# Opening of a transformer block: three products of the first scale half on VectorE, and two weight tiles loaded ahead of the second scale half

## The chip, the cores and the metric

The kernel runs on one core of one Trainium2 chip. The metric is device time in microseconds (us), the median of several executions. TensorE is PE in all rows, VectorE is DVE, ScalarE is ACT, GpSimd is POOL, and SyncE is SP.

## The reference, cut to what matters

The block takes x (512 tokens by 1024 channels) and one conditioning vector c, all float32. It is a feed-forward layer, a mixer of attention heads, and a second feed-forward layer. Each of the three normalizes its input and modulates it. The opening concerns the first one only:

```python
cond  = silu(c)                                   # 1024 values
ada   = cond @ w_ada + b_ada                      # 9 blocks of 1024: shift, scale, gate of three layers
h     = rmsnorm(x, g) * (1.0 + scale) + shift     # g: g_ffn1
gate, up = split(h @ w_up, 2)                     # 1024 -> 2 * 2816
x     = x + 0.5 * gate_0 * ((silu(gate) * up) @ w_down)
```

So nothing of the first weight product can be made before shift and scale of its channels are there, and these need 1024 by 2048 values of w_ada, 8 MB.

## The kernel before, in words

**Precision.** A float32 weight tile of 128 columns is split into a high part (`w_hi`, rounded by ACT) and a low part (`w_lo`, the rest, by DVE), and so is h (`h_hi`, `h_lo`). Each product is then three matmuls of 512 columns (`three`, lines 885 to 889). A tile is `[128, 8, 128]`: all eight groups of 128 channels for 128 output columns.

**Shift and scale in four pieces.** The 1024 channels are worked in two halves of 512. `load_piece(p)` (line 781) loads one quarter of the first two blocks of `w_ada` with four DMAs of 512 KB, each holding two of the eight groups of input channels. The pieces are called `SCALE_A`, `SCALE_B`, `SHIFT_A` and `SHIFT_B`; A is the half of channels 0 to 511. There are two ways in which the sum over the 1024 input channels is made:

- Shift, on DVE: `piece_product` (line 1944) multiplies 128 by 512 values by one column of `cond` and adds to `ada_acc`, eight times. Then `shift_columns` on PE (line 911) sums over the partitions, by four float32 matmuls of the accumulator with a column of ones. One float32 matmul stands in the trace as two records.
- Scale, on PE: `scale_row` (line 894) is a float32 matmul of 128 by 512 for each of the eight groups, with `cond` as the stationary operand. ACT copies the row that comes out (`keep_line`, line 1544). `scale_columns` (line 903) turns it into a column with four small matmuls.

DVE adds the bias (`piece_sum`, line 1957), makes the amplitude (`first_amp`, line 1962), and then `h_full` and `h_low_first` on DVE and `h_first` on ACT make `h_hi` and `h_lo` of one group of 128 channels after the other.

**The order of the opening** is written out by hand on each queue, and each engine does its list strictly in order:

- SP issues the DMAs: x in four, SHIFT_A, SCALE_A, SCALE_B (four each), the weight tiles 0, 1 and 2 (`load_up_first`, line 771), SHIFT_B, tile 3 (lines 788 to 796).
- PE transposes x, and x scaled by its norm (`turn_xr`), with the eight products of SCALE_A among them. Then come `shift_columns(SHIFT_A)`, the first product of SCALE_B, `scale_columns(SCALE_A)`, the last two `turn_xr`, and products 1 to 5 of SCALE_B (lines 968 to 983). A product of even number waits for its DMA (line 897). Then the weight tiles 0 and 1 with groups 0 to 3 (lines 993 to 998), products 6 and 7 of SCALE_B, tiles 2 and 3, and after them groups 4 to 7.
- ACT copies the transposes out, keeps the line, and makes `h_hi` of groups 0 to 3 with the high parts of tiles 0 and 1 in between (lines 1562 to 1575).
- DVE makes the eight products of SHIFT_A, the sums, then `h` of groups 0 to 3 with the low parts of tiles 0 and 1 in between (lines 2114 to 2131), then the products of SHIFT_B.

PE starts a weight tile only when `w_lo` of it is there (`split_ready`, line 891). After the opening, PE works through the rest of the block nearly without pause.

Of the kernel before, what the change touches and what calls it, by code (L numbers as in the profile page):

```python
# [5 lines left out]
ALU = mybir.AluOpType  # L6
# [7 lines left out]
P = 128  # L14
SEQ = 512
TB = SEQ // P
D = 1024
KC = D // P
# [13 lines left out]
B_LOOP = 2  # L32
XR_BANK = (5, 6, 7, 0, 1, 2, 3, 0)
SCALE_A, SCALE_B, SHIFT_A, SHIFT_B = range(4)
UP_BLOCKS = (FC - 2) // 4
DOWN_CHUNKS = (3, 3, 2, 0)

# [263 lines left out]
def hybrid_block_kernel(  # L301
# [4 lines left out]
    with ctx:  # L306
        def sem(name):
            return ctx.enter_context(nc.semaphore(name))
# [14 lines left out]
        def keep(name, shape, dt=F32):  # L323
# [17 lines left out]
        ones = keep("ones", [P, 1])  # L341
# [6 lines left out]
        cond = keep("cond", [P, KC])  # L348
# [19 lines left out]
        ada_acc = at("ada_acc", [P, D], F32, region + 2 * FC * SEQ * 4 + 2 * D * 4)  # L368
# [6 lines left out]
        ada_first = at("ada_first", [P, 4, KC, SEQ], F32, region + 2 * TB * D * 4)  # L375
# [79 lines left out]
        bank = [ctx.enter_context(nc.psum_tensor(f"bank{i}", [P, SEQ], F32)) for i in range(8)]  # L455
# [4 lines left out]
        piece_in, up_in = block_in, block_in[0:3]  # L460
# [20 lines left out]
        silu_done, hid_f32, hid_hi_done, hid_done = (  # L481
            sem("silu_done"), sem("hid_f32"), sem("hid_hi_done"), sem("hid_done"))
        mix_zero, k_zero = sem("mix_zero"), sem("k_zero")
        k_twice = [sem("k_twice0"), sem("k_twice1")]
        wf_split, wf_split_hi, f_logit, f_sum, f_act, f_dve = (
            sem("wf_split"), sem("wf_split_hi"), sem("f_logit"), sem("f_sum"), sem("f_act"), sem("f_dve"))
# [272 lines left out]
        def _(sp):  # L759
# [11 lines left out]
            def load_up_first(n):  # L771

                c0 = n // 2 * P + n % 2 * FFN
                sp.dma_start(tile8(w_raw, n), up_v[0][:, :, c0:c0 + P]).then_inc(w_in_sem[n], 16)
# [6 lines left out]
            def load_piece(p):  # L781

                c0 = (p < 2) * D + p % 2 * SEQ
                for n in range(KC // 2):
                    sp.dma_start(ada_first[:, p, 2 * n:2 * n + 2, :], ada_v[:, 2 * n:2 * n + 2, c0:c0 + SEQ])\
                      .then_inc(piece_in[p][n], 16)
# [2 lines left out]
                sp.dma_start(x_nat[:, tb, :], x[0, tb * P:(tb + 1) * P, :]).then_inc(x_in[tb], 16)  # L789
            load_piece(SHIFT_A)  # L790
            load_piece(SCALE_A)
            load_piece(SCALE_B)
            for n in range(3):
                load_up_first(n)
            load_piece(SHIFT_B)
            load_up_first(3)
            sp.dma_start(b_f[:], b_forget.rearrange("o h -> h o")).then_inc(fbias_in, 16)
# [84 lines left out]
        def _(pe):  # L882
            mm = nc.tensor.matmul
# [10 lines left out]
            def scale_row(p, k):  # L894

                if k % 2 == 0:
                    pe.wait_ge(piece_in[p][k // 2], 16)
                last = mm(bank[4 + p][:], cond[:, k:k + 1].broadcast_to([P, P]), ada_first[:, p, k, :],  # L898
                          start=k == 0, stop=k == KC - 1)
                if k == KC - 1:  # L900
                    last.then_inc(row_up, 1)

            def scale_columns(p):

                pe.wait_ge(row_kept, p + 1)
                for j in range(4):
                    last = mm(bank[7 - 3 * p][:, j:j + 1], scale_line[0:1, p, j * P:(j + 1) * P], ones[0:1, :],
                              start=True, stop=True)
                last.then_inc(ada_col, 1)

            def shift_columns(p):
# [56 lines left out]
            for k in range(3):  # L968
                turn_xr(k)
            pe.wait_ge(cond_ready, 1)  # L970
            for k in range(KC):
                scale_row(SCALE_A, k)
                if k < 3:
                    turn_xr(k + 3)
# [33 lines left out]
            for k in range(4, KC):  # L1008
                pe.wait_ge(h_done, k + 1)
                for n in range(2):  # L1010
                    last = tile_chunk(T_UP1, n, k, w2_hi, w2_lo)
                    if k == KC - 1:
                        last.then_inc(w_used, 1)
            for n in range(2, 4):
                for k in range(4, KC):
                    last = tile_chunk(T_UP1, n, k, w2_hi, w2_lo)
# [44 lines left out]
            n = KC - 1  # L1061
# [4 lines left out]
            for k in range(DOWN_PARTS[0][1]):  # L1066
                for h in range(2):
                    last = three(side_bank[h], tile8(w_hi, t % 2)[:, k, :], tile8(w_lo, t % 2)[:, k, :],
                                 hid_hi[:, k, side(h)], hid_lo[:, k, side(h)], k == 0, False)
# [44 lines left out]
            for k in range(KC):  # L1114
                pe.wait_ge(h_done, KC + k + 1)
                for i in range(2):
                    last = first_tiles(i, k, 1)
# [280 lines left out]
        def _(act):  # L1398
# [131 lines left out]
            def keep_xr(k):  # L1530

                act.wait_ge(xr_turned, k + 1)
                if k == 0:
                    act.wait_ge(x_turned, KC)
                a(xr[:, k, :], bank[XR_BANK[k]][:], ACT.Copy).then_inc(xr_ready, 1)

            def split_up(n):

                act.wait_ge(w_in_sem[n], 16)
                if n == 2:  # L1540
                    act.wait_ge(xr_turned, KC)
                a((w_hi if n < 2 else w2_hi)[:, n % SPLIT, :], w_raw[:, n, :], ACT.Copy).then_inc(w_hi_done, 1)

            def keep_line(p):

                act.wait_ge(row_up, p + 1)
                a(scale_line[0:1, p, :], bank[4 + p][0:1, :], ACT.Copy).then_inc(row_kept, 1)

            def h_first(k):

                act.wait_ge(ada_out, 2 if k < 4 else 4)
                act.wait_ge(amp_done, 1 if k < 4 else 2)
                a(h_hi[:, k, :], xr[:, k, :], ACT.Identity, bias=ada[:, k:k + 1], scale=amp[:, k:k + 1])\
                    .then_inc(h_hi_done, 1)
# [6 lines left out]

            for k in range(6):
                keep_xr(k)
            keep_line(SCALE_A)
            h_first(0)
            keep_xr(6)
            h_first(1)
            keep_xr(7)
            split_up(0)
            h_first(2)  # L1570
            split_up(1)
            h_first(3)
            split_up(2)
            split_up(3)
# [329 lines left out]
        def _(dve):  # L1904
# [39 lines left out]
            def piece_product(p, k):  # L1944

                c0 = p % 2 * SEQ
                if k % 2 == 0:
                    dve.wait_ge(piece_in[p][k // 2], 16)
                if k == 0:
                    ins = v.tensor_scalar(ada_acc[:, c0:c0 + SEQ], ada_first[:, p, 0, :], cond[:, 0:1], None, ALU.mult)  # L1950
                else:
                    dve.wait_ge(ada_mul, KC * (p - 2) + k)
                    ins = v.scalar_tensor_tensor(ada_acc[:, c0:c0 + SEQ], ada_first[:, p, k, :], cond[:, k:k + 1],
                                                 ada_acc[:, c0:c0 + SEQ], ALU.mult, ALU.add)
                ins.then_inc(ada_mul, 1)

            def piece_sum(order, c0, b):

                dve.wait_ge(ada_col, order)
                v.tensor_tensor(ada[:, c0:c0 + 4], bank[b][:, 0:4], vcol[:, c0:c0 + 4], ALU.add).then_inc(ada_out, 1)  # L1960
# [107 lines left out]
            def split_up(n):  # L2068

                dve.wait_ge(w_hi_done, n + 1)  # L2070
                hi, lo = (w_hi, w_lo) if n < 2 else (w2_hi, w2_lo)
                v.tensor_tensor(lo[:, n % SPLIT, :], w_raw[:, n, :], hi[:, n % SPLIT, :].bitcast(F32), ALU.subtract)\
                    .then_inc(w_lo_done, 1)
# [40 lines left out]
            dve.wait_ge(cond_ready, 1)  # L2114
            for k in range(KC):
                piece_product(SHIFT_A, k)
            piece_sum(1, 0, 6)
            piece_sum(2, KC, 7)
            first_amp(0)
            dve.wait_ge(amp_done, 1)  # L2120
# [3 lines left out]
            h_low_first(0)  # L2124
            h_low_first(1)
            h_full(2)
            split_up(0)
            h_low_first(2)
            split_up(1)
            h_full(3)  # L2130
            h_low_first(3)
            for k in range(4):
# [478 lines left out]
```

## Time and profile before

| what | value |
|---|---|
| median of 3 executions | 1090.0 us (1089.26 to 1090.44) |
| the profiled execution's own time | 1089.68 us |
| its span, first to last instruction | 1087.9 us |
| around the span | 1.78 us |
| PE busy | 1070.9 us, 98% |
| DVE busy | 691.8 us, 64% |
| ACT busy | 500.9 us, 46% |
| mean granted TensorE clock | 0.999 |

The profiled execution lies 0.3 us below the median. Durations in the rows further down are from this one execution. A busy share is an average over the whole span; the opening, which the change touches, is the first 50 us of it.

### The profile page before, as it was taken

The numbers are of one execution on the slowest core, as the hardware profiler recorded it, in microseconds if no ns is written. First come the engines' busy times: TensorE is split into PE (matmuls) and PEld (weight loads), VectorE is DVE, ScalarE is ACT, GpSimd is POOL, SyncE is SP. The second block draws the span as 40 slices with busy tenths as digits, with TensorE's granted clock in tenths as the row PEclk, the third lists the DMA queues.
The fourth block names the chain that finished last, engine by engine and source line by source line (L and its number), as shares of the span: only waits on it lengthen the run. The fifth ranks groups of instructions, "written<-read, shape, count | busy, mean of one in ns | idle before, by whom it ended". The sixth has DMA issues, their size and how long they took to land.

```text
span 1087.9 us, 16282 instructions
## 1 busy us (share of the span) xinstructions
PE 1070.9 (98%) x6072; PEld 911.4 (84%) x6072; DVE 691.8 (64%) x1054; ACT 500.9 (46%) x833; POOL 42.3 (4%) x76
## 2 busy tenths in 40 slices
PE   8999999999999999999999999999999999999997
PEld 5788888888878889888778777789999999978886
DVE  3755555555653557886786676678766667684343
ACT  5523222223222235776796776358544454541222
POOL 1000000000000001110111011000000000000000
PEclk9999999999999999999999999999999999999999
DMA  9868888885474552398699567246777667132221
GB/s 344 239 211 292 264 276 283 275 306 156 140 228 130 176 157 79 90 221 203 142 187 197 124 145 165 77 125 156 190 200 193 171 181 203 60 106 98 87 97 78
DMA packets 209053, 191.84 MB, mean 176 GB/s; under 512 B 7660, under 2 KB 183900, under 8 KB 206940
## 3 DMA queue, kind: packets, MB, share of 16 engines
q1 hardware_dynamic: 201392, 146.86, 45.8%
q0 software_dynamic: 7424, 44.04, 16.1%
q8 instruction: 42, 0.69, 0.3%
q14 instruction: 23, 0.19, 0.1%
q10 hardware_dynamic: 172, 0.06, 0.0%
HBM read 186.74 MB, written 44.04 MB: 212 GB/s over the span
## 4 chain that ended last, share of the span: by engine, by line
PE 89%; DVE 4%; DMA 2%; ACT 2%; issue 1%; SPq 0%; DVEq 0%; POOL 0%; ACTq 0%
PE bank L887 27%; PE bank L889 27%; PE bank L888 27%; PE bank L1246 1%; PE bank L898 1%; PE bank L1218 1%; DVE hid_lo L2066 1%; PE bank L1194 1%; PE bank L1195 1%; DMA x_nat<-in_x_dram 1%; DMA k_hh_b<-k_hh_b 0%; PE bank L924 0%; ACT w_hi L1411 0%; DMA k_hh_a<-k_hh_a 0%; DVE y L2584 0%
## 5 line engine op out<-in xcount | busy, mean ns | idle before, releaser
L887 PE MATMUL bank<-h_hi,w_hi 128*128 128x512 f32 (+1 forms) x592 | 230.3, 389 | 0.1
L889 PE MATMUL bank<-h_hi,w_lo 128*128 128x512 f32 (+1 forms) x592 | 223.5, 378 | 0.0
L888 PE MATMUL bank<-h_lo,w_hi 128*128 128x512 f32 (+1 forms) x592 | 223.5, 378 | 0.0
L1912 DVE TENSOR_TENSOR w_lo<-w_raw,w_hi 128x1024 fp32r<-128x1024 f32 x97 | 118.7, 1225 | 156.1 <-ACT w_hi L1411 155.5
L1411 ACT ACTIVATE w_hi<-w_raw 128x1024 fp32r<-128x1024 f32 x97 | 102.5, 1058 | 204.0 <-PE bank L889 179.2
L887 PEld LDWEIGHTS bank<-h_hi,w_hi 128*128 128x128 f32 x592 | 111.8, 189 | 25.5 <-issue 4.2
L888 PEld LDWEIGHTS bank<-h_lo,w_hi 128*128 128x128 f32 x592 | 111.7, 189 | 24.0 <-issue 2.9
L889 PEld LDWEIGHTS bank<-h_hi,w_lo 128*128 128x128 f32 x592 | 111.6, 189 | 22.6
L2018 DVE TENSOR_TENSOR up_lo<-up_raw,up_hi 128x1024 fp32r<-128x1024 f32 x80 | 86.6, 1085 | 21.1 <-ACT up_hi L1480 21.1
L889 PE MATMUL bank<-combo,up_lo 128*128 128x256 f32 x320 | 90.6, 283 | 0.0
L887 PE MATMUL bank<-combo,up_hi 128*128 128x256 f32 x320 | 90.6, 283 | 0.0
L888 PE MATMUL bank<-combo,up_hi 128*128 128x256 f32 x320 | 90.2, 282 | 0.0
L1480 ACT ACTIVATE up_hi<-up_raw 128x1024 fp32r<-128x1024 f32 x80 | 75.2, 943 | 0.0
L887 PE MATMUL bank<-hid_hi,w_hi 128*128 128x512 f32 (+1 forms) x198 | 74.0, 374 | 1.0 <-DVE w_lo L1912 1.0
L889 PE MATMUL bank<-hid_hi,w_lo 128*128 128x512 f32 (+1 forms) x198 | 73.5, 371 | 0.0
L888 PE MATMUL bank<-hid_lo,w_hi 128*128 128x512 f32 (+1 forms) x198 | 73.4, 371 | 0.0
L889 PE MATMUL bank<-w_hi,hid_lo 128*128 128x512 f32 x176 | 69.8, 396 | 0.0
L887 PE MATMUL bank<-h_hi,up_hi 128*128 128x256 f32 x240 | 68.0, 283 | 0.0
L888 PE MATMUL bank<-h_lo,up_hi 128*128 128x256 f32 x240 | 67.7, 282 | 0.0
L889 PE MATMUL bank<-h_hi,up_lo 128*128 128x256 f32 x240 | 67.6, 282 | 0.0
L1421 ACT ACTIVATE w_hi<-down_raw 128x1024 fp32r<-128x1024 f32 (+1 forms) x24 | 23.7, 987 | 86.6 <-PE bank L889 82.0
L1941 DVE SCALAR_TENSOR_TENSOR ada_acc<-ada_w,cond,ada_acc 128x1024 f32<-128x1024 f32 x49 | 62.6, 1278 | 0.0
(274 smaller groups left out, 2173.5 us busy)
## 6 DMA issues: line engine op xcount, KB each, us to landing
w_sums<-in_w_ffn_up_dram POOLq DMA_DIRECT2D x24, 1280.0 KB, 8.9
ada_w<-in_w_ada_dram SPq DMA_DIRECT2D x56, 512.0 KB, 3.8
w_raw<-in_w_ffn_up_dram SPq DMA_DIRECT2D x48, 512.0 KB, 7.2
up_raw<-w_sums SPq DMA_DIRECT2D x40, 512.0 KB, 5.5
w_raw<-in_w_in_dram SPq DMA_DIRECT2D x28, 512.0 KB, 3.8
w_sums<-w_sums POOLq DMA_DIRECT2D x8, 1280.0 KB, 10.3
up_raw<-in_w_ffn_up_dram SPq DMA_DIRECT2D x20, 512.0 KB, 4.1
down_raw<-in_w_ffn_down_dram SPq DMA_DIRECT2D x20, 512.0 KB, 3.7
```

The lines of the kernel that those rows point to most:

```text
L887: mm(dst, wh, xh, start=start, stop=False, skip_group_check=skip)
L888: mm(dst, wh, xl, start=False, stop=False, skip_group_check=skip)
L889: return mm(dst, wl, xh, start=False, stop=stop, skip_group_check=skip)
L898: last = mm(bank[4 + p][:], cond[:, k:k + 1].broadcast_to([P, P]), ada_first[:, p, k, :], start=k == 0, stop=k == KC - 1)
L1194: mm(zb[:, c0:c0 + n], qs, k_hh[j % 2][:, h, 0:n], start=True, stop=False)
L1195: mm(zb[:, c0:c0 + n], qs, k_l[j % 2][:, h, 0:n], start=False, stop=False)
L1411: a(w_hi[:, s, :], w_raw[:, r, :], ACT.Copy).then_inc(w_hi_done, 1)
L1421: a(w_hi[:, t % SPLIT, 0:n], down_raw[:, t % RAW, 0:n], ACT.Copy).then_inc(w_hi_done, 1)
L1480: a(up_hi[f % 2][q][:], up_raw[n % 3][q][:], ACT.Copy).then_inc(w_hi_done, 1)
L1912: v.tensor_tensor(w_lo[:, s, :], w_raw[:, r, :], w_hi[:, s, :].bitcast(F32), ALU.subtract)\
L1941: ins = v.scalar_tensor_tensor(ada_acc[:], source, cond[:, k:k + 1], ada_acc[:], ALU.mult, ALU.add)
L2018: v.tensor_tensor(up_lo[s][q][:], up_raw[s][q][:], up_hi[f % 2][q][:].bitcast(F32), ALU.subtract)\
```

## The change

It has three parts. PE makes the first five of the eight products of SCALE_A; DVE makes the other three after those of SHIFT_A, in the second half of `ada_acc`. `scale_columns(SCALE_A)` waits for them on a new semaphore and sums them over the partitions with four more float32 matmuls, into the same bank columns. SP issues the weight tiles 0 and 1 between SCALE_A and SCALE_B. ACT and DVE split tiles 0 and 1 before they make h, not between the groups of h.

```diff
+ON_PE = (5, 8)
@@ semaphores
+        scale_rest = sem("scale_rest")
@@ SP
             load_piece(SHIFT_A)
             load_piece(SCALE_A)
+            load_up_first(0)
+            load_up_first(1)
             load_piece(SCALE_B)
-            for n in range(3):
-                load_up_first(n)
+            load_up_first(2)
             load_piece(SHIFT_B)
             load_up_first(3)
@@ PE, scale_row
                 last = mm(bank[4 + p][:], cond[:, k:k + 1].broadcast_to([P, P]), ada_first[:, p, k, :],
-                          start=k == 0, stop=k == KC - 1)
-                if k == KC - 1:
+                          start=k == 0, stop=k == ON_PE[p] - 1)
+                if k == ON_PE[p] - 1:
                     last.then_inc(row_up, 1)
@@ PE, scale_columns
                 pe.wait_ge(row_kept, p + 1)
+                if p == SCALE_A:
+                    pe.wait_ge(scale_rest, KC - ON_PE[p])
                 for j in range(4):
                     last = mm(bank[7 - 3 * p][:, j:j + 1], scale_line[0:1, p, j * P:(j + 1) * P], ones[0:1, :],
-                              start=True, stop=True)
+                              start=True, stop=p == SCALE_B)
+                    if p == SCALE_A:
+                        last = mm(bank[7][:, j:j + 1], ada_acc[:, SEQ + j * P:SEQ + (j + 1) * P], ones[:],
+                                  start=False, stop=True)
                 last.then_inc(ada_col, 1)
@@ PE
-            for k in range(KC):
+            for k in range(ON_PE[SCALE_A]):
                 scale_row(SCALE_A, k)
                 if k < 3:
                     turn_xr(k + 3)
@@ ACT
             for k in range(6):
                 keep_xr(k)
+            split_up(0)
             keep_line(SCALE_A)
+            split_up(1)
             h_first(0)
             keep_xr(6)
             h_first(1)
             keep_xr(7)
-            split_up(0)
             h_first(2)
-            split_up(1)
             h_first(3)
@@ DVE
+            def scale_rest_product(k):
+
+                acc = ada_acc[:, SEQ:2 * SEQ]
+                if k == ON_PE[SCALE_A]:
+                    dve.wait_ge(piece_in[SCALE_A][k // 2], 16)
+                    ins = v.tensor_scalar(acc, ada_first[:, SCALE_A, k, :], cond[:, k:k + 1], None, ALU.mult)
+                else:
+                    if k % 2 == 0:
+                        dve.wait_ge(piece_in[SCALE_A][k // 2], 16)
+                    dve.wait_ge(scale_rest, k - ON_PE[SCALE_A])
+                    ins = v.scalar_tensor_tensor(acc, ada_first[:, SCALE_A, k, :], cond[:, k:k + 1], acc, ALU.mult, ALU.add)
+                ins.then_inc(scale_rest, 1)
@@ DVE
                 piece_product(SHIFT_A, k)
+            for k in range(ON_PE[SCALE_A], KC):
+                scale_rest_product(k)
             piece_sum(1, 0, 6)
+            split_up(0)
+            split_up(1)
             piece_sum(2, KC, 7)
             first_amp(0)
@@ DVE
             h_full(2)
-            split_up(0)
             h_low_first(2)
-            split_up(1)
             h_full(3)
             h_low_first(3)
```

## Rows read from the trace of the kernel before

**Rows 1.** The page: PE's busy time, and the chain that ended last, by engine.
```profile
PE 1070.9 (98%) x6072; PEld 911.4 (84%) x6072; DVE 691.8 (64%) x1054; ACT 500.9 (46%) x833; POOL 42.3 (4%) x76
...
PE 89%; DVE 4%; DMA 2%; ACT 2%; issue 1%; SPq 0%; DVEq 0%; POOL 0%; ACTq 0%
```

**Rows 2.** Busy time by stretch: us, engines' busy (instructions), granted clock, DMA share, GB/s.
```profile
40.00:60.00 20.00, 20.00 (x94) 16.24 (x93) 11.57 (x20) 8.03 (x11) 0.12 (x1) 1.00 0.55 159
...
500.00:800.00 300.00, 295.93 (x1804) 254.33 (x1803) 222.29 (x427) 199.18 (x376) 19.17 (x24) 1.00 0.67 155
```

**Rows 3.** Timeline of PE, 20 to 33 us: start us, length us, what.
```profile
20.16 4.46 PE L898 MATMUL bank<-ada_first,cond 128*128 128x512 f32 x10
...
24.45 0.95 PE L915 MATMUL bank<-ones,ada_acc 128*128 128x1 f32 x8
...
25.26 1.10 PE L898 MATMUL bank<-ada_first,cond 128*128 128x512 f32 x2
...
26.30 1.05 PE L907 MATMUL bank<-ones,scale_line 1*128 1x1 f32 x8
...
27.27 1.09 PE L956 MATMUL bank<-ident,xr_nat 128*128 128x128 f32 x8
...
32.67 0.47 PE L887 MATMUL bank<-h_hi,w_hi 128*128 128x512 f32 x1
```

**Rows 4.** Timeline of SP's queue, five of its issues: start us, length us.
```profile
8.78 1.17 SPq L785 DMA_DIRECT2D ada_first<-in_w_ada_dram  x1
...
13.80 1.23 SPq L785 DMA_DIRECT2D ada_first<-in_w_ada_dram  x1
...
15.59 6.46 SPq L774 DMA_DIRECT2D w_raw<-in_w_ffn_up_dram  x1
...
22.09 3.40 SPq L774 DMA_DIRECT2D w_raw<-in_w_ffn_up_dram  x1
...
25.54 2.40 SPq L785 DMA_DIRECT2D ada_first<-in_w_ada_dram  x1
```

**Rows 5.** DMA issues, the same five in the same order: us from issue to landing.
```profile
ada_first<-in_w_ada_dram SPq DMA_DIRECT2D x1, 512.0 KB, 11.3
...
ada_first<-in_w_ada_dram SPq DMA_DIRECT2D x1, 512.0 KB, 11.9
...
w_raw<-in_w_ffn_up_dram SPq DMA_DIRECT2D x1, 512.0 KB, 14.3
...
w_raw<-in_w_ffn_up_dram SPq DMA_DIRECT2D x1, 512.0 KB, 9.4
...
ada_first<-in_w_ada_dram SPq DMA_DIRECT2D x1, 512.0 KB, 7.4
```

**Rows 6.** Timeline of DVE, 15 to 35 us (in brackets: idle before, and its releaser).
```profile
15.67 5.68 DVE L1953 SCALAR_TENSOR_TENSOR ada_acc<-ada_first,cond,ada_acc 128x512 f32<-128x512 f32 x7
...
25.44 0.16 DVE L1960 TENSOR_TENSOR ada<-bank,vcol 128x4 f32<-128x4 f32 x1 [4.09 <-PE bank L915]
...
27.38 0.16 DVE L1960 TENSOR_TENSOR ada<-bank,vcol 128x4 f32<-128x4 f32 x1 [1.78 <-PE bank L907]
...
33.04 1.22 DVE L2072 TENSOR_TENSOR w_lo<-w_raw,w_hi 128x1024 fp32r<-128x1024 f32 x1
```

**Rows 7.** Timeline of PE, where tile 0 ends and tile 1 begins.
```profile
33.91 0.40 PE L889 MATMUL bank<-h_hi,w_lo 128*128 128x512 f32 x1
...
34.41 0.47 PE L887 MATMUL bank<-h_hi,w_hi 128*128 128x512 f32 x1
```

**Rows 8.** Timeline of PE, its first matmuls: bf16, 512 columns each.
```profile
2.23 5.05 PE L931 MATMUL bank<-ident_bf 128*128 128x512 bf16 x12 [2.23 <-POOL ident_bf L652]
...
7.23 0.81 PE L931 MATMUL bank<-ident_bf 128*128 128x512 bf16 x3
```

**Rows 9.** Busy time by stretch after the last matmul, columns as in Rows 2.
```profile
1082.00:1083.00 1.00, 0.04 (x1) 0.00 (x0) 1.00 (x2) 0.89 (x3) 0.00 (x0) 1.00 0.94 385
...
1085.00:1086.00 1.00, 0.00 (x0) 0.00 (x0) 0.00 (x0) 0.00 (x0) 0.00 (x0) 0.76 0.89 356
```

## The prediction

> **What bounds the kernel now.** I read the page first, for what limits the whole. PE is busy for 98% of the span and holds 89% of the chain that ended last [rows 1]. Then the table by stretch, to see from where that holds: from 40 us on PE is busy all of the time, and in the mixer in all but 4 us of 300 [rows 2]. So once the first weight tiles run, the rest of the kernel is a block of PE work of fixed length, and a change of the opening is worth the time by which that block starts earlier or later, no more.
>
> Then PE's own timeline of the opening, read backwards from the first weight matmul at 32.67 us [rows 3]. Products 1 to 5 of SCALE_B and two groups of transposes stand right before it, with no idle worth the name, back to 27.27. Before those is `scale_columns(SCALE_A)` at 26.30, before that the first product of SCALE_B at 25.26, the shift columns at 24.45, and the tail of SCALE_A's products: five of them from 20.16, so (24.45 - 20.16) / 5 = 0.86 us each. PE's list is thus a chain without slack, from which 3 products could be taken. Last I read SP's queue with the landings [rows 4, 5], because PE's list holds waits for DMAs, and the change moves two of them. Issue plus time to landing gives: last quarter of SCALE_A 8.78 + 11.3 = 20.1; last quarter of SCALE_B 25.7; tile 1 29.9; tile 2 31.5; first quarter of SHIFT_B 32.9. SCALE_B's own four lie between 20.1 and 25.7, 1.4 us apart, so its first quarter lands at 21.5 now, 3.8 us before PE asks for it. That slack is what the change spends.
>
> **Part 1, three products off PE.** PE saves 3 x 0.86 = 2.57 us. The shift columns then start at 21.9 instead of 24.45, take 24.45 to 25.26 = 0.81 [rows 3], and end at 22.7. SHIFT_A's products on DVE, for which they wait, end at 15.67 + 5.68 = 21.35 [rows 6], just in time.
>
> **Part 2, the same products on DVE.** Seven of the form took 5.68 us, 0.81 each [rows 6]. Three more from 21.35 end by 23.8; the first, without an addition, is if anything shorter. DVE was idle there for 4.09 us before the sum at 25.44 [rows 6], so the work is hidden. Without that cover it would cost at most 2.4 us. What waits for it is `scale_columns(SCALE_A)`, which comes to it at 26.8 by the reckoning below, so the new wait on `scale_rest` is free with 3 us to spare.
>
> **Part 3, the columns.** `scale_columns(SCALE_A)` gets four more float32 matmuls with a column of ones, eight records. The same eight in the shift columns took 0.81 us [rows 3]. They stand on the chain: DVE's sum of the scale follows them (27.38 now, [rows 6]), and so do the last transposes and the products of SCALE_B. They replace 2.57 us, but 0.81 comes back. Bounds: 0.4 if they slip under the others' weight loads, 1.6 if one-row and full loads in turn cost double. I take 0.81, the row with the same form.
>
> **Part 4, the DMAs, on which it turns.** Tiles 0 and 1 together took from 25.7 to 29.9, 4.2 us, more than the 2.8 us that two quarters of a piece take [rows 4, 5]. Put behind SCALE_A, they land by 20.1 + 4.2 = 24.3, and the first quarter of SCALE_B follows 1.4 us later (as SHIFT_B's first did behind tile 2), at 25.7. The queue's issue does not make it later: tile 1 would be issued from about 10.5 for 6.46 us, to 17.0, and a quarter issued then needs 7.4 us if nothing stands in front [rows 4, 5], 24.4. It does not run dry either. But PE's second item behind the shift columns is the first product of SCALE_B, and it waits for that landing. So PE arrives at 22.7 and stands until 25.7, and `scale_columns(SCALE_A)`, the transposes and all the rest are queued behind it. The product starts near 25.8 where it was 25.26: 0.54 later, not 2.57 earlier. Everything that the DVE products won is idle time of PE, and a little more. Bounds for the landing: 24.3 if a tile costs no more than a quarter (1.4 each), 26.7 if each costs as much as the first of a run can have cost, 4.2 less the 1.6 from tile 1 to tile 2, so 2.6 each.
>
> The Trainium skill speaks to the lower bound ("DMA: Bandwidth & Descriptors", Specifications): it has rows of at least 512 bytes moving at line rate, and a tile's rows are exactly 512 bytes, a piece's 2048. By that rule the sum would be the first rival's, below. The trace does not agree: 4.2 us for two tiles against 2.8 for two quarters.
>
> **Part 5, the splits moved.** ACT makes the high part of tile 0 when it lands, near the middle between 20.1 and 24.3, keeps the line by 24, then tile 1; DVE makes the low parts between the two sums. All four are done by 27, before the amplitude can be there, so they cost nothing, and free ACT and DVE later. What they hid before was one stall: tile 1's low part was written from 33.04 to 34.26 [rows 6], and PE's next matmul, due 0.24 after the one at 33.91, came at 34.41 [rows 7]. That gives back 34.41 - 34.15 = 0.26 us. What comes next there is not late: h of groups 0 to 3 moves with the columns, as PE does, and now has fewer things between its steps. Tile 2 and SHIFT_B land as before, since the bytes ahead of them are the same, and PE comes to them later.
>
> **The sum.** +0.54 (waiting for SCALE_B) + 0.81 (more columns) - 0.26 (the stall before tile 1) = +1.1 us at the first weight tiles, and the block behind is moved by as much. Against the profiled execution: 1089.68 + 1.1 = 1090.8; that one was 0.3 below the median, so the median forecast is 1090.0 + 1.1 = **1091.1 us**. With the bounds: 24.3 for the landing and 0.4 for the columns give -0.86 + 0.4 - 0.26 = -0.7, and 26.7 with 1.6 gives +1.5 + 1.6 - 0.26 = +2.9, so 1089.3 to 1092.9. About 0.2%, 2.2 us, is what a measurement of this kernel can tell from no change; 1087.8 to 1092.2 counts as the same.
>
> **Rivals.**
>
> *The tiles move as fast as the pieces.* SCALE_B's first quarter lands at 24.3. PE starts the product 0.86 earlier than before, loses 0.81 to the columns and wins 0.26: -0.3, 1089.7 us. For it: a queue that is kept full might have hidden some of the 4.2 us as a one-time start-up at the change of row length. Against: the measured landings. Chance 0.12.
>
> *The full gain.* PE does not stand at all: product at 22.7, columns 1.04 later at 23.7 as now, 0.97 + 0.81 long, to 25.5 where it was 27.27, -1.8, and -0.26: -2.0, 1088.0 us. It needs the first quarter of SCALE_B at 22.7 with 1 MB more in front of it, 3 us sooner than the rows allow. Chance 0.03. Even it would be barely outside of the same.
>
> *The clock falls, slower.* PE stands from 22.7 to 25.8, 3.1 us, after 0.8 us of matmuls of one column. At the end of the kernel the last matmul ended at 1082.04, and the granted clock went from 1.00 to 0.50 within 1085 to 1086; a mean of 0.76 over that us puts it at 1085.5, 3.5 us after [rows 9]. The new pause is shorter than that; counted from the last wide matmul, at 21.9, it is 3.9 and longer. If it falls here, PE goes on at 1.2 GHz, the lower level, until it has been at work again. The price is in PE's first matmuls: 12 took 5.05 us, 0.42 each, where the three that follow took 0.27 each with the end of the last in it; at twice the clock the 12 take half, so 2.5 us are lost [rows 8]. Together +3.6, 1093.6 us, outside of the same. It decides from the point at which the clock falls before 25.8. For it: the nearness of 3.1 and 3.9 to 3.5. Against: by the time without any matmul the pause stays short of the only one that is known to be enough. Chance 0.13.
>
> The Trainium skill ("TensorE: Matmul & The Clock Gate", What's actually happening) calls the throttled clock the default that activity lifts, and says that idling brings it back. The fall at the kernel's end agrees; that a pause as short as this one is enough, which by the rule would give this rival's time, no row here shows.
>
> *The change does not do what it says*: DVE's three products come too late and PE waits for them instead. They would have to end after 26.8, 3 us later than worked out. It and all else that I have not seen: 0.04.
>
> **How the numbers follow.** My forecast has 0.68, and its own range is 1089.3 to 1092.9. The first rival lies within it. With the spread of the executions, range 1089.2 to 1092.9: the full gain, the clock and the unseen are left out, 0.20. Slower by over 0.2%: the clock 0.13, and 0.02 of the forecast's upper tail. Faster: the better part of the full gain and some of the unseen, 0.04. The same: 0.81.
>
> **What would show it.** Right: PE's first product of SCALE_B starts at 25.6 to 26.0 after some 3 us of idle put down to a DMA of `ada_first`; the columns last 1.8 us; the scale's sum on DVE at 28.7; the first weight matmul near 34.0, with no stall before tile 1; granted clock 1.00 throughout. Wrong: the first product at 24.5 or before (tiles load faster), the first weight matmul before 32.7, a granted clock of 0.50 after 24 us, or a first weight matmul near 34 and yet a time below 1090, which would mean that the block behind it isn't fixed.

## The result, and the profile after

The changed kernel takes 1094.58 us (median of 6 executions, 1092.14 to 1094.87) beside 1090.05 us before: a ratio of 1.0037, 95% interval 1.0027 to 1.0046. It is slower by 4.0 us by the ratio and by 4.5 by the medians; the interval lies well above 1. The forecast was 1091.1 us and no change; the time lies outside of the range. The rival named "the clock falls" gave 1093.6 us and had a chance of 0.13. One execution of the kernel before, in a later session, ran at a mean clock of 0.75 and took 1302.98 us; it is left out of all comparisons and spreads below.

The page of the changed kernel: the span, then PE's busy time.

```profile
span 1091.6 us, 16291 instructions
...
PE 1073.8 (98%) x6074; PEld 914.8 (84%) x6074; DVE 694.0 (64%) x1057; ACT 501.1 (46%) x833; POOL 42.5 (4%) x76
```

This profiled execution took 1093.35 us. PE is busy for 98% as in [rows 1], and for 2.9 us more, though three products of 0.86 us were taken from it. So look at the opening. PE's timeline of the changed kernel (start us, length us, what; line numbers are those of the changed kernel, L903 is `scale_row`, L914 and L917 the two matmuls of `scale_columns`, L925 the shift columns, L966 `turn_xr`):

```profile
20.01 1.88 PE L903 MATMUL bank<-ada_first,cond 128*128 128x512 f32 x4
21.73 0.95 PE L925 MATMUL bank<-ones,ada_acc 128*128 128x1 f32 x8
24.77 2.07 PE L903 MATMUL bank<-ada_first,cond 128*128 128x512 f32 x2 [2.10 <-DMA ada_first<-in_w_ada_dram]
26.77 0.58 PE L914 MATMUL bank<-ones,scale_line 1*128 1x1 f32 x2
27.29 0.59 PE L917 MATMUL bank<-ones,ada_acc 128*128 128x1 f32 x2
...
30.82 1.95 PE L966 MATMUL bank<-ident,xr_nat 128*128 128x128 f32 x8
32.55 5.37 PE L903 MATMUL bank<-ada_first,cond 128*128 128x512 f32 x10
...
43.37 1.88 PE L903 MATMUL bank<-ada_first,cond 128*128 128x512 f32 x4
```

Against [rows 3]: the shift columns begin at 21.73 where it was 24.45, so the three products are gone as meant. Then PE stands for 2.10 us, put down to the DMA of `ada_first`. The first product of SCALE_B begins at 24.77 (25.26 before), and takes 2.07 us where it took 1.10. What follows is slow too: the columns (the matmuls of `scale_columns(SCALE_A)`) start at 26.77 and end at 30.82, where the eight records before took 0.97 us in all, and the transposes take 1.95 us where they took 1.09. The table by stretch, with the granted clock as the third figure from the end, says why (one engine's busy time first):

```profile
23.00:24.00 1.00, 0.00 (x0) 1.00 1.04 383
24.00:25.00 1.00, 0.23 (x1) 0.57 1.06 391
25.00:26.00 1.00, 1.00 (x2) 0.50 1.04 387
...
33.00:34.00 1.00, 1.00 (x2) 0.50 1.03 381
34.00:36.00 2.00, 2.00 (x5) 0.91 1.09 348
```

TensorE's clock falls from 2.4 to 1.2 GHz just after 24 us, 2.4 us after the last wide product gave way to the shift columns at 21.73, and within the pause. (A mean of 0.57 over the stretch from 24 to 25 puts it at 24.1.) It comes back at about 34.4: ten us at half the clock. The kernel before holds 1.00 through all of the opening.

A good mark for the whole opening is the place at which products 6 and 7 of SCALE_B begin, behind tiles 0 and 1: 38.70 before, 43.37 now, 4.67 us later. The row of the kernel before, for comparison with all that follows:

```profile
38.70 1.88 PE L898 MATMUL bank<-ada_first,cond 128*128 128x512 f32 x4
```

The span is longer by only 3.7; 0.9 of the difference lies in the mixer, where PE waited for two DMAs of `k_hh` for 2.3 us before and 1.4 us now. This wait differs by execution: over all profiles of this document it is between 1.2 and 2.9 us. PE's waits in the kernel before, then in the changed kernel (us in total, times, longest):

```profile
PE bank L1194 <- DMA k_hh_b<-k_hh_b: 1.3, 1, 1.3
PE bank L1194 <- DMA k_hh_a<-k_hh_a: 1.0, 1, 1.0
```

```profile
PE bank L903 <- DMA ada_first<-in_w_ada_dram: 2.1, 1, 2.1
...
PE bank L1204 <- DMA k_hh_a<-k_hh_a: 0.9, 1, 0.9
...
PE bank L1204 <- DMA k_hh_b<-k_hh_b: 0.5, 1, 0.5
```

Last the DMAs. The first quarter of SCALE_B in the changed kernel, its issue on SP's queue, then its time to landing:

```profile
16.05 3.56 SPq L789 DMA_DIRECT2D ada_first<-in_w_ada_dram  x1
```

```profile
ada_first<-in_w_ada_dram SPq DMA_DIRECT2D x1, 512.0 KB, 8.7
```

It lands at 16.05 + 8.7 = 24.75; the forecast had 25.7. The last quarter of SCALE_A landed at 8.34 + 11.4 = 19.7, so the two tiles and this quarter took 5.0 us. Tile 1 was issued at 10.96 and landed 12.4 us later, at 23.4, so the tiles took 3.6 of it.

### The profile page after: what moved, and what is told of

Its sections match the earlier page's. It is cut to its first block, busy times and chain, and to the rows that moved or that the text cites. A ratio compares the mean times of both kernels' runs of the same rounds, so it can differ in the third digit from the quotient of the medians.

```text
span 1091.6 us, 16291 instructions
## 1 busy us (share of the span) xinstructions
PE 1073.8 (98%) x6074; PEld 914.8 (84%) x6074; DVE 694.0 (64%) x1057; ACT 501.1 (46%) x833; POOL 42.5 (4%) x76
## 4 chain that ended last, share of the span: by engine, by line
PE 87%; DVE 4%; DMA 3%; ACT 2%; SPq 1%; issue 1%; DVEq 0%; POOL 0%; ACTq 0%
PE bank L892 27%; PE bank L893 27%; PE bank L894 27%; PE bank L1256 1%; PE bank L1228 1%; DVE hid_lo L2089 1%; PE bank L1204 1%; DMA w_raw<-in_w_ffn_down_dram 1%; PE bank L903 1%; DMA ada_first<-in_w_ada_dram 1%; PE bank L1205 1%; SPq L789 1%; SPq L778 1%; ACT w_hi L1421 1%; PE bank L934 0%
```

## The experiments

Theory 1: PE's list has a pause between the shift columns and the first product of SCALE_B, among matmuls of one column; the clock falls in it, and the low clock is what costs. Theory 2: the path itself is longer, by slow small matmuls and moved DMAs, and the clock has no part in it. In all runs below the mark is the start of products 6 and 7 of SCALE_B.

**Filling the pause (e1_fill9, e4_fill3).**

```diff
             shift_columns(SHIFT_A)
+            warm(9, 5)        # e4_fill3: warm(3, 5)
             scale_row(SCALE_B, 0)
```

> The changed kernel with nine bf16 matmuls of 512 columns (0.22 us each, into a bank that nobody needs) between the shift columns and the first product of SCALE_B, so that PE works through the pause in which it waits for SCALE_B. Theory 1 (the pause lets the clock fall, and the low clock is what costs): granted clock 1.00 throughout, first product of SCALE_B near 24.8, first weight matmul near 33.0, time about 1090.3. Theory 2 (the path itself is longer: sixteen small matmuls in turn are slow, whatever the clock): no better than the changed kernel, 1094 or more, first weight matmul after 36.

> As the run with nine filling matmuls, but with three (0.65 us), so that a pause of about 1.4 us without any matmul stays. Theory 1, if a pause this short is not enough: clock 1.00, 1090.3. Theory 1, if little work in that stretch counts as none: the clock falls in some or all executions, 1092 to 1095, and the executions differ among each other by more than those of the kernel before. Theory 2: 1094 or more.

With nine: 1091.62 us (11 executions), ratio 1.0014 (1.0005 to 1.0023), and the profiled execution took 1089.65 us at a clock of 0.999. Its timeline:

```profile
22.46 2.10 PE L941 MATMUL bank<-ident_bf 128*128 128x512 bf16 x9
24.47 1.12 PE L903 MATMUL bank<-ada_first,cond 128*128 128x512 f32 x2
25.53 0.38 PE L914 MATMUL bank<-ones,scale_line 1*128 1x1 f32 x2
...
27.70 0.38 PE L917 MATMUL bank<-ones,ada_acc 128*128 128x1 f32 x2
27.94 1.07 PE L966 MATMUL bank<-ident,xr_nat 128*128 128x128 f32 x8
28.85 4.46 PE L903 MATMUL bank<-ada_first,cond 128*128 128x512 f32 x10
38.76 1.88 PE L903 MATMUL bank<-ada_first,cond 128*128 128x512 f32 x4
```

Its table by stretch (PE's busy time, then the granted clock):

```profile
20.00:30.00 10.00, 10.00 (x51) 1.00 1.10 347
30.00:40.00 10.00, 10.00 (x35) 1.00 0.77 243
```

Work that nobody needs took 3 us off the median (2.5 by the ratios, each to the kernel before in its own session), where theory 2 had 1094 us or more. The kernel is otherwise the same, so these 14.29 us from the first product of SCALE_B to the mark (24.47 to 38.76), beside 18.60 in the changed kernel (24.77 to 43.37), are the price of the clock in that execution: 4.3 us. It also shows a term that was mis-sized: the columns take 2.41 us at the full clock (25.53 to 27.94), 1.44 more than before, not 0.81. The median is above the expected 1090.3: eight of the 11 executions had a mean clock of 0.996 or 0.997, so it probably fell somewhere in those too; where, the second profile below was meant to tell.

With three: 1093.20 us (11 executions), ratio 1.0025 (1.0016 to 1.0035). The executions lie 4.3 us apart, which is not more than the 4.9 of the kernel before in the same session, though the second form of theory 1 expected more. A pause of 1.5 us was left, and the clock fell, later:

```profile
24.57 1.12 PE L903 MATMUL bank<-ada_first,cond 128*128 128x512 f32 x2 [1.49 <-DMA ada_first<-in_w_ada_dram]
...
42.07 1.88 PE L903 MATMUL bank<-ada_first,cond 128*128 128x512 f32 x4
```

The table by stretch of that run has 1.00 to 27, 0.51 in 27 to 28 and 0.57 in 33 to 34. At 27 PE was at work on the columns without a pause, so it need not be standing still when the clock falls. Theory 1 as first put, a fall "in the pause", is too narrow: here the fall came 2.5 us after the pause had ended, behind one wide product and four of the eight pairs of records of the columns.

**The two halves of the change, each alone (e2_products_only, e3_tiles_only).** The first restores the order of DMAs and of splits; the second gives PE its eight products back.

```diff
# e2_products_only: SP, ACT and DVE lists as before the change, products and columns as after it
# e3_tiles_only
-ON_PE = (5, 8)
+ON_PE = (8, 8)
@@ scale_columns as before the change
```

> The changed kernel with the DMA order and the split order of the kernel before: only the three products on DVE and the four more column matmuls remain. Theory 1: SCALE_B is there when PE asks for it (it landed at 21.5 before), no pause, granted clock 1.00, columns from 23.7, 1.8 us long, first weight matmul near 30.9, the splits of tiles 0 and 1 are now the next to be late (tile 1 up to 32.5), so 1.5 to 2 us below the kernel before: 1088.3. Theory 2 (the columns are slow in themselves): columns 4 us long, first weight matmul near 33, 1091.

> Only the DMAs and the splits moved; PE makes all eight products of SCALE_A. PE then asks for SCALE_B at 25.2, and it lands at 24.8. Theory 1: no pause, clock 1.00, one stall of 0.26 less before tile 1: 1089.8. Theory 2: also no pause; this run tells the two apart only by excluding that the moved tiles cost something of their own, in which case it would be above 1091.

The products alone: 1090.10 us (11 executions), ratio 1.0001 (0.9993 to 1.0010), where theory 1 had 1088.3. PE had no pause: shift columns at 21.48, the product at 22.29, the columns from 23.33. And yet:

```profile
25.00:26.00 1.00, 1.00 (x7) 0.82 1.20 290
26.00:27.00 1.00, 1.00 (x6) 0.50 1.20 291
...
28.00:29.00 1.00, 1.00 (x2) 0.50 1.15 297
29.00:30.00 1.00, 1.00 (x3) 0.98 1.12 336
```

The clock fell at 25.6 with PE busy all of the time, in the last pair of the sixteen small records. So in this execution it took no pause: between 21.48 and the fall PE made the shift columns, one wide product and the columns. The low clock lasted 3.4 us, shorter than in the changed kernel. The product began 2.97 us earlier than in the kernel before and the mark came at 38.21, only 0.49 earlier; of the 2.48 us between, 1.44 is the longer columns and about 1.0 the low clock. Not all executions show it: two of the 11 had a mean clock of 1.000, and they were the fastest, 1088.95 and 1089.21 us, still above the 1088.3 expected.

The tiles alone: 1089.02 us (12 executions; 1089.8 expected), ratio 0.9990 (0.9980 to 1.0000). PE asked for SCALE_B at 25.43, when it was there (landed at 25.2). The way from there to the mark is 12.84 us (38.27 - 25.43) beside 13.44 before (38.70 - 25.26). So having the splits done early is worth 0.6 us, not the 0.26 of the one visible stall. The profiled execution is the slowest of the twelve, 1093.63 us. Its clock held up to the mark and was low twice behind it: from 45.3 to 48.7, after the small matmuls of the second half (`scale_columns(SCALE_B)` and `shift_columns(SHIFT_B)`, up to 44.74), and from 308.1 to 311.5.

**Only a pause, in the kernel before (e8_pause_only, e9_fill_only).** Nothing of the change is in these.

```diff
             shift_columns(SHIFT_A)
+            pe.wait_ge(w_in_sem[0], 16)     # e9_fill_only: warm(12, 5)
             scale_row(SCALE_B, 0)
```

> The kernel before, and nothing of the change: only PE waits for the landing of tile 0 (28.0) ahead of the first product of SCALE_B, a pause of 2.7 us. Theory 1 (the pause lets the clock fall): the path gets 2.7 us longer and the clock takes 1.7 to 4 us more, so 1094.8 to 1097, mean granted clock 0.994 to 0.997 in nearly all executions. Theory 2 (the pause costs its own length and no more): 1093.1, clock as in the kernel before.

> The kernel before with twelve wide bf16 matmuls in that place, 2.6 us of work instead of 2.7 us of pause. Both theories: 2.6 us longer, 1093.0, clock as in the kernel before or higher. The difference between this run and the one with the pause is the price of the clock in this stretch: 0 by theory 2, 1.7 to 4 us by theory 1.

With the pause 1095.29 us (5 executions, ratio 1.0037, 1.0023 to 1.0051), with work in its place 1093.61 us (11 executions, ratio 1.0013, 1.0002 to 1.0024). The pause came out at 3.3 us, longer than the 2.7 expected and than the 2.1 of the changed kernel. First the one with the pause, then the one with work:

```profile
28.04 2.07 PE L898 MATMUL bank<-ada_first,cond 128*128 128x512 f32 x2 [3.29 <-DMA w_raw<-in_w_ffn_up_dram]
30.04 1.86 PE L907 MATMUL bank<-ones,scale_line 1*128 1x1 f32 x8
...
45.09 1.88 PE L898 MATMUL bank<-ada_first,cond 128*128 128x512 f32 x4
```

```profile
27.23 1.02 PE L898 MATMUL bank<-ada_first,cond 128*128 128x512 f32 x2
28.18 1.05 PE L907 MATMUL bank<-ones,scale_line 1*128 1x1 f32 x8
...
40.58 1.88 PE L898 MATMUL bank<-ada_first,cond 128*128 128x512 f32 x4
```

The same instructions take 17.05 us from the first product to the mark after a pause, and 13.35 after work: 3.7 us for the clock, in a kernel without the three DVE products and without the longer columns. That is what theory 2 forbids. The clock fell at about 26.5, within the pause, and came back at 36.8 (means of 0.76 from 26 to 27 and 0.62 from 36 to 37). The medians are only 1.7 us apart, the lower edge of what was expected. One reason is a second place, near 300 us, told of in the next paragraph. Of the 11 executions with work in the pause, seven have a mean clock of 0.997 or 0.998 and took 1093.4 to 1094.1 us, and four took 1091.3 to 1091.6; the profiled one is of the seven, and its clock was low from 308.9 to 312.3. That this place makes up the whole of the difference is not shown.

**Second profiles (e10_changed_again, e11_fill9_again, e12_before_again).** The kernels are unchanged.

> The changed kernel once more, for a second profile and more executions beside those of the kernel before. Theory 1: the clock falls in every execution, mean granted clock 0.994 to 0.997, median 1094.5, and the time of an execution goes with its mean clock. Theory 2: time and mean clock have nothing to do with each other.

> The run with nine filling matmuls once more, for a second profile: its executions had a mean clock of 0.997 in most cases, and one profile cannot say where the clock fell in those. If the small matmuls of the opening are enough by themselves, this profile shows a granted clock below 1.00 between 24 and 34 us; if they are not, it shows it elsewhere (near 300 us, where the first feed-forward layer ends) or not at all.

> The kernel before once more, for a second profile. Theory 1: no fall in the opening, where its longest stretch of small matmuls has a wide product in the middle; a fall near 300 us is possible.

The changed kernel: 1095.12 us, ratio 1.0036 (1.0023 to 1.0049), mean clock 0.994 or 0.995 in all six. In its profile the clock fell later than in the first, after a pause of 2.32 us in which it had held, and the mark is at 42.05:

```profile
26.00:27.00 1.00, 1.00 (x8) 0.89 1.05 383
27.00:28.00 1.00, 1.00 (x6) 0.50 1.03 367
...
33.00:34.00 1.00, 1.00 (x3) 0.70 1.02 377
```

From the product to the mark it is 17.44 us (24.61 to 42.05), 3.15 more than at the full clock. This execution had a second low stretch behind the mark, from 310.1 to 313.5, which the first profile has not. So in both profiles of the changed kernel the clock fell in the opening, at a moment that varied, and the price was 3.15 and 4.3 us. The mean clocks of all 12 executions are 0.994 to 0.996, those of the kernel before 0.996 to 1.000; this fits a fall in the opening each time, and is not a proof of it, since a mean clock names no place. That the time of an execution goes with its mean clock, as was expected, does not hold among these six: the two at 0.995 took 1095.37 and 1096.07, the four at 0.994 took less or about the same.

The run with nine filling matmuls showed no fall in the opening, nor near 300 us, in its second profile either (one execution, mark at 38.78, 1091.01 us, mean clock 0.998), so what lowers the clock in its executions at 0.996 and 0.997 stays open. Its two profiles are 1.36 us apart with the mark in the same place and no fall before the last matmul; 1.2 of this is the wait for `k_hh`, 1.2 us in the first and 2.4 in the second. The second profile of the kernel before has none there, but one elsewhere (1092.6 us):

```profile
300.00:305.00 5.00, 3.55 (x16) 1.00 1.05 330
305.00:310.00 5.00, 4.19 (x12) 0.67 0.44 124
```

There the first feed-forward layer ends and PE has idle time. So the kernel before, too, has a place where the clock falls in some executions. Its executions spread from 1088.8 to 1094.4 us; this place and the wait for `k_hh` (2.3 us in its first profile, 2.9 in its second) both take part in that, by how much is not shown. It is also why a mean clock of 0.997 does not say where the fall was.

**The columns in two groups (e7_fill9_grouped).**

```diff
-                for j in range(4):   # per j: scale_line matmul, then ada_acc matmul
+                for j in range(4):   # four scale_line matmuls (the first of them with start=True)
+                for j in range(4):   # then four ada_acc matmuls
```

> As the run with nine filling matmuls, with the sixteen column records in two groups of eight instead of in turn. If turning between one-row and full operands is what makes them take 2.4 us, they take 1.8 now, and products 6 and 7 come at 38.2 instead of 38.8. Theory 1: the stretch of small matmuls is shorter, the clock falls in fewer executions, median 1090.0 to 1090.8 instead of 1091.6. Theory 2: only the 0.6 us, 1091.0.

1091.26 us (12 executions), ratio 1.0006 (0.9994 to 1.0017).

```profile
25.65 1.05 PE L912 MATMUL bank<-ones,scale_line 1*128 1x1 f32 x8
26.63 1.05 PE L917 MATMUL bank<-ones,ada_acc 128*128 128x1 f32 x8
27.54 1.07 PE L966 MATMUL bank<-ident,xr_nat 128*128 128x128 f32 x8
```

The sixteen records take 1.89 us instead of 2.41, and 0.92 more than the eight before. So turning between one-row and full operands costs 0.52 us, 0.13 for each of the four pairs. The mark came 0.41 earlier than in the run that alternates. The median did not go where it was forecast (1090.0 to 1090.8); its executions fall into two bunches, five of 1088.9 to 1089.6 and seven of 1090.9 to 1093.6, and the profiled one, of the second bunch, has its fall near 307 us, none in the opening.

**The change without its pause (e5_quarter_first, e6_quarter_two).** SP issues the first quarter of SCALE_B ahead of the two tiles and the other three behind them. The columns are grouped, ACT keeps the line before it splits, and DVE makes tile 1's low part after `h_full` of the first two groups.

```diff
             load_piece(SCALE_A)
+            load_quarter(SCALE_B, 0)
             load_up_first(0)
             load_up_first(1)
-            load_piece(SCALE_B)
+            for n in range(1, KC // 2):
+                load_quarter(SCALE_B, n)
@@ ACT
-            split_up(0)
             keep_line(SCALE_A)
+            split_up(0)
             split_up(1)
@@ DVE
             split_up(0)
-            split_up(1)
             piece_sum(2, KC, 7)
...
             h_full(1)
+            split_up(1)
@@ PE, e6_quarter_two only
             scale_row(SCALE_B, 0)
+            scale_row(SCALE_B, 1)
             scale_columns(SCALE_A)
```

> The changed kernel with the first quarter of SCALE_B issued ahead of tiles 0 and 1 (its other three quarters behind them), the two kinds of column matmuls one after the other instead of in turn, and the line kept before the splits. PE should not pause at all. Theory 1, as it stands now: the clock falls when a stretch of PE holds little but matmuls of one column; that stretch is shorter here (3.5 us with one product in it). With the clock at 1.00: first product of SCALE_B at 22.5, columns 1.8 us long to 25.3, products 6 and 7 of SCALE_B near 36.2 (38.70 before), 1087.6. If the clock still falls in most executions, for one step of 3.4 us: 1.7 us more, 1089.3. Theory 2 (the moved tiles or the three products on DVE cost something beyond the pause and the clock): 1091 or more.

> As the run before it, and the second product of SCALE_B is made before the columns rather than after them, so 0.86 us of wide work goes into the stretch of small matmuls. The columns come 0.86 later, which the two products that follow less hide. Theory 1: the clock falls in fewer executions than without that, and the median is at or below 1087.8. Theory 2 (time follows the columns, not the clock): 0.9 us slower than the run before it.

The first: 1089.05 us (12 executions), ratio 0.9984 (0.9975 to 0.9992). It beats the kernel before by 1.7 us by the ratio and, by over 5 us, the changed one. Its timeline:

```profile
21.89 0.95 PE L931 MATMUL bank<-ones,ada_acc 128*128 128x1 f32 x8
22.70 1.11 PE L909 MATMUL bank<-ada_first,cond 128*128 128x512 f32 x2
23.74 1.05 PE L918 MATMUL bank<-ones,scale_line 1*128 1x1 f32 x8
24.72 1.05 PE L923 MATMUL bank<-ones,ada_acc 128*128 128x1 f32 x8
25.63 1.07 PE L972 MATMUL bank<-ident,xr_nat 128*128 128x128 f32 x8
26.54 4.46 PE L909 MATMUL bank<-ada_first,cond 128*128 128x512 f32 x10
36.45 1.88 PE L909 MATMUL bank<-ada_first,cond 128*128 128x512 f32 x4
```

No pause, no fall, the mark at 36.45, 2.25 us earlier than in the kernel before, and 1087.59 us for that execution; the reckoning had 36.2 and 1087.6. The median is 1.5 us above, at mean clocks of 0.997 to 1.000. So with the first quarter issued in time, the columns in groups and the splits in another order, the idea of the change is worth some 2 us. What each of the three gives was not measured alone; the first is why PE no longer waits (the quarter landed at 9.50 + 11.4 = 20.9), and by the run before this one the second is worth some 0.5 us.

The second: 1088.97 us, ratio 0.9985 (0.9976 to 0.9995), no better. The product ahead of the columns cost nothing (mark at 35.94), which speaks against theory 2, but did not raise the clock, which speaks against what theory 1 expected of it. In its profile the clock was low from 43.3, 0.5 us behind the small matmuls of the second half, to 46.7; that edit does not touch them, and the run with the tiles alone was low in nearly the same place. How often the fall is in one place or the other, single profiles do not tell.

## Why the prediction was wrong

**The step that failed** is the weighing in "The clock falls, slower": "by the time without any matmul the pause stays short of the only one that is known to be enough". The pause was 2.10 us, shorter still than the 3.1 reckoned, and the clock fell, so the term for the clock in the sum, put at nothing, was 4.31 us. The pause at the kernel's end [rows 9] was read as a threshold; it is one pause that was enough, and gives no lower bound. The length of the pause was also not all there was to weigh. With three filling matmuls the clock fell at 27 us, among the columns and with the pause over, and with the products alone it fell without any pause. In all of these PE had made little but matmuls one column wide, or stood, since the shift columns, with at most one wide product (and three filling matmuls) in between. The forecast named the shift columns and the pause, and left out the columns behind the product, though it had itself made them longer. The rival's mechanism was therefore right as to place and sign, at a chance of 0.13 that was too low, and its price was too low as well: 2.5 us forecast from PE's first matmuls [rows 8], 4.3 and 3.15 us measured in the two profiles, in which the clock stayed down for ten and seven us, through the columns and transposes. That the rival's 1093.6 us lies within 1 us of the result is in part luck: it adds a price that was too small to a path that was reckoned too long (+1.1 us, measured +0.36). Why the same list of small matmuls brings a fall in one execution and none in another stays open.

The Trainium skill ("TensorE: Matmul & The Clock Gate", What's actually happening) had the throttled clock as the default that activity lifts. The run with the products alone agrees with that sentence: its clock fell at 25.6 us while PE was busy for all of the time.

**The rest of the sum**, with the full clock of e1_fill9 and of e3_tiles_only as the measure:

| term | forecast | measured |
|---|---|---|
| first product of SCALE_B, from its landing | +0.54 | -0.49 (24.77 - 25.26) |
| columns | +0.81 | +1.44 (2.41 - 0.97) |
| splits done early | -0.26 | -0.59 (14.29 - 13.44 - 1.44) |
| clock | 0 | +4.31 (18.60 - 14.29) |
| at the mark | +1.1 | +4.67 |

So without the clock the change would have come out at +0.36 us at the mark: no change, as forecast, but by luck, from three terms that were each off by half or more and offset one another. The run with nine filling matmuls, which has these terms without the pause, came out higher in the median, +1.5 us; of that, no profile shows the cause.

- Part 1 was right: shift columns at 21.73, forecast 21.9. Of the gain of the three products, 2.6 us, 2.1 went into a wait for the first quarter of SCALE_B, which was the central claim.
- Part 2 was right: DVE's three products ended at 23.24, and nobody waited for them.
- Part 3 was mis-sized, 1.44 us for 0.81. The row it was taken from has eight matmuls of one form in a run; the change puts them in turn with others. The grouped run gave 0.92, near the 0.81; the alternation gives the rest. It was within the bounds.
- Part 4 was right in kind and off by 1 us: landing at 24.75. The tiles took 3.6 us together, not 4.2, and the whole opening ran 0.4 us earlier. By the Trainium skill's rule of line rate from 512 bytes ("DMA: Bandwidth & Descriptors", Specifications) the tiles would take 2.8 us; the trace does not agree, with 3.6 here and again with the tiles alone.
- Part 5 read the one gap between tile 0 and tile 1. The run with the tiles alone shows 0.6 us for the same part. That the rest comes from smaller gaps as tile 0 begins was not looked at further.
- That the block behind the opening keeps its length held between these two profiles: 4.67 at the mark less 0.9 for the two `k_hh` waits is 3.8, against a span 3.7 longer. From execution to execution it does not: the `k_hh` waits and the low clock near 300 us move it by as much as the forecast's whole sum.

## What to carry to other kernels

When work is taken from an engine, read what its next item waits for before counting the gain: here one DMA queued behind two others turned most of 2.6 us of saved work into a pause, and with its first quarter issued in time the same idea, somewhat reordered, was a gain. Where a trace shows TensorE pausing or at work on matmuls one column wide, judge the stretch as a whole and not by its longest gap: here the clock fell with pauses of 3.3, 2.1, 1.5 and 0 us in it. Needless wide matmuls in the pause were cheaper than the low clock (1091.62 against 1094.58 us). One pause that was enough says nothing of shorter ones; a forecast that rests on staying below it needs a run of its own.

## What the runs showed of the hardware that was not expected

- The granted clock fell from 1.00 to 0.50 with PE busy all of the time, in sixteen records of float32 matmuls one column wide (at 25.6 us in e2_products_only, back at 29.0), after a pause of 1.49 us with three wide matmuls ahead of it (at 27.0 in e4_fill3), and within a pause of 2.10 us (at 24.1 in the changed kernel). The moment differed between two profiles of the same kernel: 24.1 and 26.8. With the same records and no pause it did not fall in the opening of e1_fill9, e5_quarter_first, e7_fill9_grouped or e11_fill9_again.
- The same sixteen records took 2.41 us in turn, 1.89 us in two groups.
- Once fallen, the clock stayed at 0.50 for three to ten us in the opening, also while PE made wide products.
- The kernel before had a fall of its own near 306 us in one of its two profiles, and so had four of the variants (e3_tiles_only, e7_fill9_grouped, e9_fill_only, e10_changed_again) between 307 and 310 us. Its executions spread over 3.2 to 5.6 us in a session, those of the variants over 2.1 to 5.3, more than the three of the start (1089.26 to 1090.44) had let one think.
